# One projected tile's filler steps moved from the B heads into the A heads of an attention stage, on one Trainium2 core

## The chip, the cores and the metric

The kernel runs on one core of one Trainium2 chip. The metric is device time in microseconds (us) of one execution. Engines: TensorE (PE) multiplies matrices, VectorE (DVE) and ScalarE (ACT) do elementwise work and copies, GpSimd (POOL) adds and multiplies on the side, SyncE (SP) issues DMA loads and stores. PSUM is the memory that matmuls write, here eight banks.

## The reference, cut to what matters

One inference step of a one-layer encoder for 512 prompt frames and 64 new ones (576 tokens): a feed-forward network, an attention layer with two groups of heads, a second feed-forward network, a final norm.

```python
proj = u @ w_in                       # queries, keys, values of both groups
qa, ka, va, qb, kb, vb = jnp.split(proj, cuts, axis=-1)
qa, ka, qb, kb = rope(...)            # rotary
oa = swa_prompt(qa, ka, va, sinks)    # group A: chunk window, learned sinks
ob = diff_prompt(qb, kb, vb, lam)     # group B: softmax of map 1 - lam * softmax of map 2
h = h + jnp.concatenate([oa, ob], axis=-1) @ w_out
```

The 64 new frames do the same against a cache (`swa_sample`, `diff_sample`).

## The kernel before, in words

Products are exact to fp32 by three passes: each weight block is split into w_hi (a copy by ACT, `hi_block` L1334) and w_lo (a subtraction by DVE, `lo_block` L1855), and a step multiplies hi by hi, hi by lo and lo by hi for two halves of the tokens: six matmuls of 288 columns.

The projections of queries and keys are 13 tiles in the order ka, qa0 to qa3, kb0, qb0, kb1, qb1, kb2, qb2, kb3, qb3 (`TILES`, numbers 0 to 12), eight steps each (`tile_step` L1069). Every tile from qa1 on is accumulated in the same two PSUM banks. When a tile's eighth step is done, DVE takes it out (`take_projection` L2235: a shuffle, L2244, and a multiplication, L2246, which frees the banks); then POOL does the rotary (L2550, L2500) and, for a query tile, writes the new frames' part into a small tile q_diag (L2580). So:

- the first step of tile b waits until DVE has taken tile b - 1 (L1081);
- the take of tile b waits until POOL has finished the rotary of tile b - 1 (L2242), because both use the same two buffers;
- a rotary that writes into a slot waits until all scores that read the slot's former tile are made: q and k slots go by the head's number, even or odd (L2564), q_diag's two slots by the tile's number, even or odd (L2574 to L2577);
- the scores of a head wait for its tiles' rotary.

The attention is made of units: for each A pair t the units (A,t,0), (A,t,1) for the prompt and (As,t,0) for the new frames; for each B head h (Bs,h,0), (B,h,0) to (B,h,3), and L(Lh,0), which turns the head's output back. A unit is scored on PE (S), its maxima are found on DVE (`maxima` L2282), exponentials are made on ACT (`exps` L1691), probabilities are scaled on DVE (N, `normalise` L2318). Then it goes through one or two of 40 rounds, numbered 0 to 39: in round r PE transposes the probabilities (T r), ACT copies them (`copy_turned` L1723), and PE multiplies them with the values (O r). T r waits for the copy of T r-1. Rounds 0 to 19 are the A pairs (five for each: two for each A unit, one for As), rounds 20 to 39 the B heads. The outputs of an A pair are put by DVE into the mixing tiles (`outputs` L2352); B heads have a norm (R), scaled by ACT (L1775) before L.

Between these PE does filler steps, of the tiles first and then of the output projection. `make_schedule` (L254) writes all this as one list of events, which every engine follows in its own program order, so an instruction that waits holds all that stands behind it on that engine. `FILL` (L68) has for each round the number of steps after T r and its scores, and after O r; `FILL_START` (L67) the steps before round 0. `ACT_SPLITS` and `DVE_SPLITS` (L69, L70) say how many events of other kinds after the first step of tile b - 2 (or block) the w_hi and w_lo of block b stand. A few units' exponentials come late (`ACT_LATE`, L82): those of (A,2,0) stand behind the copy of T9.

SP loads each tile's 512 KB of weights into one of three slots, when the split of the block three before is done; stores of the rotated keys stand in the same queue, that of kb0 between the loads of qb1 and kb2, that of kb1 between those of qb2 and kb3, that of kb2 after that of qb3.

Of the kernel before, what the change touches and what calls it, by code (L numbers as in the profile page):

```python
# [63 lines left out]


LEAD = 2
FILL_START = (1, 6)  # L67
FILL = ((1, 0), (2, 0), (3, 0), (3, 0), (1, 4), (1, 0), (1, 0), (1, 0), (3, 0), (0, 3), (1, 0), (0, 0), (1, 0), (0, 3), (3, 0), (1, 1), (0, 3), (2, 1), (2, 0), (3, 3), (0, 2), (0, 2), (4, 2), (0, 5), (3, 0), (1, 2), (3, 2), (4, 2), (2, 0), (3, 1), (0, 0), (2, 2), (3, 0), (0, 1), (3, 0), (1, 1), (2, 1), (1, 3), (4, 0), (3, 9))  # L68
ACT_SPLITS = (4, 0, 4, 0, 0, 0, 2, 1, 3, 0, 3, 0, 7, 2, 0, 7)  # L69
DVE_SPLITS = (7, 17, 8, 6, 8, 0, 4, 2, 4, 10, 8, 0, 9, 9, 1, 21)  # L70
ACT_ROOTS = (1, 0, 0, 0)
ACT_SCALES = (0, 2, 2, 0)
ACT_TILES = (0, 0, 0, 3)
# [180 lines left out]
def make_schedule():  # L254
# [24 lines left out]
    def fill(n):  # L279

        for _ in range(n):
            step()

    def score(n):
        kind, t, _ = units[n]
        last = TILES.index(f"qa{t}" if kind[0] == "A" else f"qb{t}")

        while done[0] < (last + 1) * KD + (LEAD if n > 1 else 0) and step():
            pass
        events.append(("S", n))  # L290
# [3 lines left out]
    score(0)  # L294
    fill(FILL_START[0])
    score(1)
    events.append(("N", 0))
    fill(FILL_START[1])
    waiting = []
    for at, n in enumerate(scored):  # L300
        kind, head, i = units[n]
        parts = 2 if kind == "A" else 1
        for part in range(parts):
# [3 lines left out]
            if part == parts - 1:  # L307
# [4 lines left out]
                if at + 2 < len(scored) and at not in SCORES_FIRST:  # L312
                    score(scored[at + 2])
            fill(FILL[r][0])
            events.append(("O", r))
            fill(FILL[r][1])

# [17 lines left out]
def with_splits(places):  # L335

    out, owed = [], []
    for e in EVENTS:
        if e[0] == "k" and e[2] == 0 and e[1] <= LAST_FILLER:
            while owed and owed[0][0] < e[1] + 1:  # L340
                out.append(("W", owed.pop(0)[0]))
        out.append(e)
        if e[0] == "k":
            if e[2] == 0 and FIRST_TILES <= e[1] <= LAST_FILLER:
                owed.append([e[1] + 2, places[e[1] - FIRST_TILES]])
        else:
            for w in owed:
                w[1] -= 1
        while owed and owed[0][1] <= 0:
            out.append(("W", owed.pop(0)[0]))  # L350
    return out + [("W", b) for b, _ in owed]


def with_first_split(events):

    at = events.index(("N", 0)) + 1
    return events[:at] + [("W", V_BLOCKS - 1)] + events[at:]


def with_roots(events, later):  # L360

    out, held = [], []
    for e in events:
        if e[0] == "R":
            held.append([e, later[UNITS[e[1]][1]]])
        else:
            out.append(e)
            if e[0] not in "kW":
                for h in held:
                    h[1] -= 1  # L370
        while held and held[0][1] <= 0:
            out.append(held.pop(0)[0])
    return out


def with_scales(events, later):

    out, held = [], []
    for e in events:
        out.append(e)  # L380
        if e[0] == "R":
            held.append([("Q", e[1]), later[UNITS[e[1]][1]]])
        elif e[0] not in "kW":
            for h in held:
                h[1] -= 1
        while held and held[0][1] <= 0:
            out.append(held.pop(0)[0])
    return out


def with_late_scores(events, late):

    out, held = [], []
    for e in events:
        if e[0] == "S" and e[1] in late:
            held.append(e)
            continue
        out.append(e)
        if e[0] == "T":
            out += held  # L400
            held = []
    return out


ACT_EVENTS = with_scales(with_late_scores(with_roots(with_splits(ACT_SPLITS), ACT_ROOTS), ACT_LATE), ACT_SCALES)
DVE_EVENTS = with_first_split(with_roots(with_splits(DVE_SPLITS), DVE_ROOTS))

# [2333 lines left out]
```

## Time and profile before

| | us |
|---|---|
| median of 3 runs | 1033.09 (1032.91 to 1033.96) |
| the profiled execution | 1034.29 |
| its span, first to last instruction | 1032.5 |
| PE busy | 1015.2 (98%) |
| DVE busy | 799.8 (77%) |
| ACT busy | 564.5 (55%) |
| POOL busy | 171.6 (17%) |

Starts are counted from the first instruction of the span. A row of a timeline gives the start, the time from there to the end of the row's last instruction, engine, line, operation, output and inputs, and how many instructions it merges; a bracket at its end says how long the engine idled before it and whose end it waited for. Matmuls overlap, so a row's time is longer than the distance to the next row.

### The profile page before, as it was taken

The page shows a single profiled execution, that of the slowest core. Times are in us where ns is not written, and L with a number is a line of the kernel's source. Part 1 is how long each engine was busy: PE and PEld are TensorE (multiplying, and loading weights), DVE is VectorE, ACT ScalarE, POOL GpSimd, SP SyncE. Part 2 cuts the span into 40 slices and gives each one's busy share as a digit, 9 for nine tenths or more (in the row PEclk, how much of TensorE's full clock was granted, in tenths as well). Part 3 has the DMA queues.
Part 4 walks back from the last instruction along what each step waited for, and adds up shares of the span by engine and source line. Part 5 has one row for each costly group of instructions (what it writes and reads, how often), then busy time and mean ns, then how long its engine had stood idle before and what let it go on. Part 6 is the DMA issues. An engine that isn't in the chain of part 4 may idle for free.

```text
span 1032.5 us, 19489 instructions
## 1 busy us (share of the span) xinstructions
PE 1015.2 (98%) x7600; PEld 989.2 (96%) x7600; DVE 799.8 (77%) x1222; ACT 564.5 (55%) x980; POOL 171.6 (17%) x296
## 2 busy tenths in 40 slices
PE   9999999999999999999999999999999999999996
PEld 9999999999999999988888899999999999999995
DVE  6998777888678895368767768698777788778884
ACT  6645554666456663345435646435654666555664
POOL 0000010010010035233544205000000010010023
PEclk9999999999999999999999999999999999999999
DMA  6436656656665536230112212316556656667542
GB/s 231 110 95 155 190 149 166 186 149 158 177 176 149 139 121 211 64 97 22 52 54 70 83 57 82 106 56 185 166 148 162 183 152 169 176 156 179 143 106 92
DMA packets 38890, 137.33 MB, mean 133 GB/s; under 512 B 5456, under 2 KB 8656, under 8 KB 38672
## 3 DMA queue, kind: packets, MB, share of 16 engines
q1 hardware_dynamic: 30736, 107.52, 30.1%
q0 software_dynamic: 8064, 28.58, 17.3%
q8 instruction: 61, 1.00, 0.4%
q14 instruction: 29, 0.24, 0.1%
HBM read 131.10 MB, written 4.98 MB: 132 GB/s over the span
## 4 chain that ended last, share of the span: by engine, by line
PE 51%; DVE 5%; issue 3%; ACT 1%; POOL 1%; DMA 1%; DVEq 0%; SPq 0%; ACTq 0%; POOLq 0%
PE acc L985 25%; PE acc L883 17%; PE acc L1120 3%; PE acc L1156 1%; PE acc L1226 1%; DVE w_lo L1853 1%; PE acc L1146 1%; DVE h_lo L1988 1%; DMA comb<-in_w2se 0%; POOL side L2520 0%; DMA raw<-in_w2se 0%; DVE res L2469 0%; POOL q_b L2500 0%; PE acc L1185 0%; PE acc L1189 0%
## 5 line engine op out<-in xcount | busy, mean ns | idle before, releaser
L985 PE MATMUL acc<-c_hi,w_lo 128*128 128x288 f32 x952 | 282.0, 296 | 0.0
L985 PE MATMUL acc<-c_hi,w_hi 128*128 128x288 f32 x952 | 281.0, 295 | 0.0
L985 PE MATMUL acc<-c_lo,w_hi 128*128 128x288 f32 x952 | 277.6, 292 | 0.0
L1853 DVE TENSOR_TENSOR w_lo<-raw,w_hi 128x1024 fp32r<-128x1024 f32 (+4 forms) x187 | 196.5, 1053 | 103.4 <-ACT w_hi L1332 87.5
L1332 ACT ACTIVATE w_hi<-raw 128x1024 fp32r<-128x1024 f32 (+4 forms) x157 | 140.7, 896 | 88.0 <-PE acc L985 57.3
L1502 ACT ACTIVATE comb<-acc 128x288 f32<-128x288 f32 x224 | 92.1, 411 | 167.3 <-PE acc L985 165.0
L985 PEld LDWEIGHTS acc<-c_lo,w_hi 128*128 128x128 f32 x952 | 180.8, 190 | 0.0
L985 PEld LDWEIGHTS acc<-c_hi,w_hi 128*128 128x128 f32 x952 | 179.0, 188 | 0.2 <-DVE w_lo L1853 0.2
L985 PEld LDWEIGHTS acc<-c_hi,w_lo 128*128 128x128 f32 x952 | 178.5, 188 | 0.0
L985 PE MATMUL acc<-h_hi,w_hi 128*128 128x288 f32 x574 | 170.8, 298 | 2.3 <-DVE h_lo L1988 0.8
L985 PE MATMUL acc<-h_hi,w_lo 128*128 128x288 f32 x574 | 169.8, 296 | 0.0
L985 PE MATMUL acc<-h_lo,w_hi 128*128 128x288 f32 x574 | 167.9, 292 | 0.0
L1853 DVE TENSOR_TENSOR w_lo<-comb,w_hi 128x1024 fp32r<-128x1024 f32 (+2 forms) x86 | 101.4, 1179 | 18.1 <-ACT w_hi L1350 15.8
L985 PEld LDWEIGHTS acc<-h_hi,w_hi 128*128 128x128 f32 x574 | 108.0, 188 | 4.8 <-DVE h_lo L1988 1.7
L985 PEld LDWEIGHTS acc<-h_lo,w_hi 128*128 128x128 f32 x574 | 108.8, 190 | 0.0
L985 PEld LDWEIGHTS acc<-h_hi,w_lo 128*128 128x128 f32 x574 | 107.8, 188 | 0.0
L883 PE MATMUL acc<-h_hi,w_hi 128*128 128x288 f32 x320 | 69.1, 297 | 0.0
L883 PE MATMUL acc<-h_hi,w_lo 128*128 128x288 f32 x320 | 68.6, 295 | 0.0
L883 PE MATMUL acc<-h_lo,w_hi 128*128 128x288 f32 x320 | 68.5, 295 | 0.0
L1356 ACT ACTIVATE w_hi<-comb 128x1024 fp32r<-128x1024 f32 (+1 forms) x56 | 58.1, 1037 | 8.3 <-PE acc L985 7.0
L2520 POOL TENSOR_TENSOR side<-side 128x576 f32<-128x576 f32 x23 | 39.6, 1720 | 81.1 <-issue 50.9
L883 PEld LDWEIGHTS acc<-h_hi,w_hi 128*128 128x128 f32 x320 | 51.8, 188 | 0.2
(257 smaller groups left out, 1831.4 us busy)
## 6 DMA issues: line engine op xcount, KB each, us to landing
raw<-in_w1st SPq DMA_DIRECT2D x17, 768.0 KB, 4.6
raw<-in_w2st SPq DMA_DIRECT2D x17, 768.0 KB, 4.3
raw<-in_w_qk SPq DMA_DIRECT2D x13, 512.0 KB, 3.7
raw<-in_w1sd SPq DMA_DIRECT2D x8, 768.0 KB, 4.2
raw<-in_w2sd SPq DMA_DIRECT2D x8, 768.0 KB, 4.3
raw<-in_w1gu SPq DMA_DIRECT2D x10, 512.0 KB, 4.6
raw<-in_w2gu SPq DMA_DIRECT2D x10, 512.0 KB, 3.8
raw<-in_w1st SPq DMA_DIRECT2D x9, 512.0 KB, 5.3
```

Source lines behind the costliest of these rows:

```text
L883: m = nc.tensor.matmul(acc[:, bank + t, 0:HALF], w_part[:, col:col + P], x_part[:, k, t * HALF:(t + 1) * HALF], start=first and n == 0, st ...
L985: m = nc.tensor.matmul(acc[:, banks[side_of(p)], 0:HALF], w_part[:, col:col + P], x_part, start=n in (P1, P5, P2) and k == 0 and e == 0, s ...
L1120: m = nc.tensor.matmul(acc[0:n_tok, V_BANK[tt], 0:V_HALF], x_part[:, kg, tok], w_part[:, split_base(key) + k * V_HALF:split_base(key) + (k ...
L1146: m = nc.tensor.matmul(acc[:, bank + e, 256 * qi + (P if tile == 0 else 0):256 * (qi + 1)], q_a[rows, t % 2, tile * P:(tile + 1) * P], k_a ...
L1156: m = nc.tensor.matmul(acc[:, bank + e, 0:(i + 1) * P], q_b[rows, t % 2, i * P:(i + 1) * P], k_b[rows, t % 2, 0:(i + 1) * P], start=True, ...
L1226: m = nc.tensor.matmul(acc[:, O_BANK, i * P:(i + 1) * P], pt[:, j * P:(j + 1) * P], v_new[:, j, b_values(t)], start=j == 0, stop=j == i)
L1332: nc.scalar.activation(cols, src, ACT.Copy).then_inc(hi_ready, 1)
L1356: nc.scalar.activation(parts_of(w_hi, P6, P3 - P6, p), w_sum[:, :, 0:width(p)], ACT.Copy).then_inc(hi_ready, 1)
L1502: nc.scalar.activation(to, acc[:, PRODUCTS[n][0][side_of(p)], 0:HALF], ACT.Copy, scale=scale).then_inc(snapped, 1)
L1853: return nc.vector.tensor_tensor(cols, src, hi.bitcast(FP32), ALU.subtract).then_inc(split_ready, 1)
L1988: nc.vector.tensor_tensor(pair_lo[:, at:at + n, :], side[:, 0:n, :], pair_hi[:, at:at + n, :].bitcast(FP32), ALU.subtract).then_inc(h_read ...
L2520: nc.gpsimd.tensor_tensor(ssq[:], ssq[:], square, ALU.add).then_inc(ssq_added, 1)
```

## The change

Eight filler steps move: `FILL_START` gets one step more and round 0 one less (qa1's last step goes ahead of T0); round 8 gets eight steps, all after O8, in place of three ahead of it; rounds 10, 11 and 12 get one more each; round 15 does its two ahead of O15; rounds 22, 23 and 26 lose three, two and three. Every tile from kb0 to kb3 ends at another place than before. Where the tile steps stand after the change, with the first steps of the next tile behind them:

```
T8 S(A2,0) O8 kb0.0-7 T9 S(A2,1) O9 qb0.0-2 T10 qb0.3-4 T11 S(As2,0) qb0.5 O11 T12 qb0.6-7
T13 S(A3,0) O13 kb1.0-2 T14 S(A3,1) kb1.3-5 O14 T15 kb1.6-7 T16 S(As3,0) O16 qb1.0-2 T17 qb1.3-4 qb1.5
T18 S(Bs0,0) qb1.6-7 O18 T19 S(B0,0) kb2.0-2 O19 kb2.3-5 T20 S(B0,1) O20 kb2.6-7 T21 S(B0,2) O21 qb2.0-1
T22 S(B0,3) qb2.2-3 O22 qb2.4 T23 S(Bs1,0) O23 qb2.5-7 T24 S(B1,0) kb3.0-2 O24 T25 S(B1,1) kb3.3 O25 kb3.4-5
T26 S(B1,2) kb3.6-7 O26 L(L0,0) T27 ...
```

From T27 on PE's list is the same as before. The w_hi of qb1 on ACT now stands between the exponentials of (A2,1) and the copy of T10. On DVE the w_lo of qb0 stands behind the take of qa3, that of kb1 ahead of the take of kb0, that of qb1 between the mixing outputs of O13 and the maxima of (A3,1), that of kb2 behind the maxima of (As3,0), that of qb2 ahead of the probabilities of (Bs0,0), that of kb3 behind the maxima of (B0,2), that of qb3 behind O24.

```diff
-FILL_START = (1, 6)
-FILL = ((1, 0), (2, 0), (3, 0), (3, 0), (1, 4), (1, 0), (1, 0), (1, 0), (3, 0), (0, 3), (1, 0), (0, 0), (1, 0), (0, 3), (3, 0), (1, 1), (0, 3), (2, 1), (2, 0), (3, 3), (0, 2), (0, 2), (4, 2), (0, 5), (3, 0), (1, 2), (3, 2), (4, 2), (2, 0), (3, 1), (0, 0), (2, 2), (3, 0), (0, 1), (3, 0), (1, 1), (2, 1), (1, 3), (4, 0), (3, 9))
+FILL_START = (1, 7)
+FILL = ((0, 0), (2, 0), (3, 0), (3, 0), (1, 4), (1, 0), (1, 0), (1, 0), (0, 8), (0, 3), (2, 0), (1, 0), (2, 0), (0, 3), (3, 0), (2, 0), (0, 3), (2, 1), (2, 0), (3, 3), (0, 2), (0, 2), (2, 1), (0, 3), (3, 0), (1, 2), (2, 0), (4, 2), (2, 0), (3, 1), (0, 0), (2, 2), (3, 0), (0, 1), (3, 0), (1, 1), (2, 1), (1, 3), (4, 0), (3, 9))
 ACT_SPLITS = (4, 0, 4, 0, 0, 0, 2, 1, 3, 0, 3, 0, 7, 2, 0, 7)
-DVE_SPLITS = (7, 17, 8, 6, 8, 0, 4, 2, 4, 10, 8, 0, 9, 9, 1, 21)
+DVE_SPLITS = (7, 17, 10, 0, 12, 10, 6, 8, 12, 14, 8, 0, 9, 9, 1, 21)
```

## Rows read from the trace of the kernel before

**Rows 1.** The page, part 1: busy time, share of the span and instructions.

```profile
PE 1015.2 (98%) x7600; PEld 989.2 (96%) x7600; DVE 799.8 (77%) x1222; ACT 564.5 (55%) x980; POOL 171.6 (17%) x296
```

**Rows 2.** The table of stretches: length, engines' busy time, PE's clock, DMA.

```profile
441.00:560.00 119.00, 114.76 (x902) 100.10 (x900) 91.04 (x234) 55.63 (x171) 52.49 (x150) 1.00 0.19 64
```

**Rows 3.** PE's timeline, rounds 1 to 18.

```profile
452.26 0.51 PE L883 MATMUL acc<-u_hi,w_hi 128*128 128x288 f32 x2 [0.91 <-DVE side L2246]
...
475.49 0.51 PE L883 MATMUL acc<-u_hi,w_hi 128*128 128x288 f32 x2 [0.16 <-DVE side L2246]
...
479.09 0.33 PE L1181 MATMUL acc<-ident,probs 128*128 128x128 f32 x1
...
484.04 0.55 PE L1178 MATMUL acc<-ident,probs 128*128 128x128 f32 x3 [0.23 <-DVE probs L2332]
...
485.63 0.52 PE L1178 MATMUL acc<-ident,probs 128*128 128x128 f32 x3 [0.25 <-ACT probs_t L1733]
...
489.42 0.63 PE L1178 MATMUL acc<-ident,probs 128*128 128x128 f32 x4 [0.43 <-ACT probs_t L1733]
...
499.25 0.55 PE L1178 MATMUL acc<-ident,probs 128*128 128x128 f32 x3 [0.46 <-DVE probs L2332]
...
501.23 0.49 PE L1178 MATMUL acc<-ident,probs 128*128 128x128 f32 x3
501.56 0.49 PE L1151 MATMUL acc<-k_all_a,q_diag 128*128 128x192 f32 x2
...
503.11 0.53 PE L883 MATMUL acc<-u_hi,w_hi 128*128 128x288 f32 x2
...
508.17 0.43 PE L883 MATMUL acc<-u_hi,w_lo 128*128 128x288 f32 x2
508.44 0.60 PE L1178 MATMUL acc<-ident,probs 128*128 128x128 f32 x4
509.90 1.24 PE L1160 MATMUL acc<-k_all_b,q_diag 128*128 128x288 f32 x4 [0.86 <-POOL q_diag L2580]
```

**Rows 4.** PE's timeline, rounds 24 to 27: T24 and a step, T26 and T27.

```profile
540.72 0.60 PE L1185 MATMUL acc<-ident,probs 128*128 128x128 f32 x4
...
541.66 0.54 PE L883 MATMUL acc<-u_hi,w_hi 128*128 128x288 f32 x2
...
550.47 0.27 PE L1185 MATMUL acc<-ident,probs 128*128 128x128 f32 x1
...
556.39 0.38 PE L1185 MATMUL acc<-ident,probs 128*128 128x128 f32 x2
```

**Rows 5.** DVE's timeline: takes, maxima, and probabilities without and beside POOL's rotary.

```profile
450.68 0.80 DVE L2244 STREAM_SHUFFLE side<-acc 128x576 f32<-128x576 f32 x1
451.37 0.74 DVE L2246 TENSOR_TENSOR side<-acc,trig 128x576 f32<-128x576 f32 x1
...
489.03 0.81 DVE L2244 STREAM_SHUFFLE side<-acc 128x576 f32<-128x576 f32 x1
...
495.95 0.27 DVE L2292 MEMSET acc<- 64x256 f32 x1 [0.40 <-PE acc L1146]
...
498.58 1.14 DVE L2332 TENSOR_SCALAR probs<-probs,st 128x256 f32<-128x256 f32 x4
...
503.38 1.79 DVE L2332 TENSOR_SCALAR probs<-probs,st 128x256 f32<-128x256 f32 x4
```

**Rows 6.** DVE's splits of tiles' weights, 441 to 560: duration in ns, least/median/most.

```profile
L1853 DVE TENSOR_TENSOR w_lo<-raw,w_hi x10: 1210/1220/1412, 448.8 to 545.7; 128x1024 fp32r<-128x1024 f32 x10
```

**Rows 7.** ACT's timeline: a w_hi split, and the scaling of head 0.

```profile
496.17 1.07 ACT L1332 ACTIVATE w_hi<-raw 128x1024 fp32r<-128x1024 f32 x1
...
552.30 1.57 ACT L1775 ACTIVATE o_b<-o_b,ss_o 128x128 f32<-128x128 f32 x5 [0.71 <-DVE ss_o L2388]
```

**Rows 8.** POOL's timeline: the rotary of qb0.

```profile
502.38 2.24 POOL L2550 TENSOR_TENSOR side<-side,trig 128x96 f32<-128x96 f32 x6 [7.61 <-DVE side L2244]
...
509.14 0.71 POOL L2580 TENSOR_TENSOR q_diag<-side 64x64 f32<-64x64 f32 x2
```

## The prediction

> **What bounds the kernel now.** I read the page first: TensorE is busy for 98% of the span [rows 1], so time can come only out of its idle spells, and go only into new ones. The table of stretches puts them in one place: between 441 and 560 us, where the attention rounds run between filler steps, PE is busy for 114.76 of 119.00 us [rows 2]. That leaves 4.24 us, the most that any order of the steps can win there. Then I read PE's timeline through this stretch [rows 3, 4] for the bracket behind a row, which says how long PE idled before it and what ended that. The reader should see three kinds of idle: a tile's first step waits until DVE has taken the former tile out of its banks (452.26, 475.49); a transpose waits for ACT's copy of the transpose before (485.63, 489.42) or for DVE's probabilities (484.04, 499.25); and one score waits for POOL's rotary (509.90). Last I read DVE, ACT and POOL at these places [rows 5 to 8]. All clocks there are granted at 1.00 [rows 2].
>
> **What moves.** Steps are dear only where they fill nothing. Two matmuls start 0.27 us apart (508.17 to 508.44) [rows 3], so a step of six costs 0.80. All 104 tile steps stay; rounds 8 (+5), 10, 11 and 12 (+1 each) get eight, rounds 22 (-3), 23 (-2) and 26 (-3) lose them. From kb0 on each tile therefore ends at another round, and with it moves everything that a tile issues: ACT's w_hi, DVE's w_lo and its two instructions of the take, POOL's fifteen pieces, SP's load. I write +x for "x us after the row that begins the round's transposes".
>
> **Gains**, each from an idle spell that a step now covers.
> (a) qa1's last step goes ahead of T0. Its take (two instructions, 450.68 to 452.11, 1.43 us [rows 5]) starts about 0.3 earlier, and qa2's wait of 0.91 [rows 3] shrinks by as much; it does not end, since T1 now waits for the copy of T0. Gain 0.3.
> (b) O8 goes between qa3's end and kb0's first step: the wait of 0.16 at 475.49 [rows 3] and a change between kinds of matmul go. Gain 0.25.
> (c) From T11 to T13 two more steps cover the copies' latencies (0.43 of idle at 489.42). T11 to T13 took 3.79 (485.63 to 489.42) [rows 3]; the work without waits, with two steps more, comes to about 4.5, in place of 3.79 + 1.6. Gain 0.9, at least the 0.43 of the idle spell.
> (d) qb0's rotary is now early, so S(Bs0,0) no longer stands 0.86 for POOL's q_diag [rows 3]. Gain 0.85.
> Together 2.3; bounds 1.7 (c at its least) and 2.7 (PE's idle at these places and what the kinds' changes add).
>
> **Losses.**
> (e) T9 to T11. T11 already waits for ACT, whose copy of T10 stands behind the exponentials. qb1's w_hi comes ahead of that copy now: a row of 1.07, about 0.95 of it not overlapped [rows 7]. One step more lies beside it. Also kb0's rotary now runs on POOL while DVE makes the probabilities of (A2,0). The four scalings took 1.14 with POOL idle and 1.79 beside POOL's rotary [rows 5, 8], 0.16 more each; with the small instructions before them I take 0.26 for ACT's start. So T9 to T11 goes from 6.54 [rows 3] to 7.75, where the step alone would make 7.34. Loss 0.4; bounds 0 (ACT's work hides) and 1.0 (no cover).
> By the Trainium skill (SBUF — State Buffer, section Who interferes with whom) the port pair of VectorE and GpSimd is an exclusive lock for a whole instruction; a scaling would then stand out a whole piece of POOL, an estimate of 2.24/6 = 0.37 in place of 0.16 [rows 8], and the time would be some 0.4 longer than my sum.
> (f) T13 to T15. DVE's chain from the take at 489.03 to its idle at 495.55 (0.40 before the row at 495.95) is 6.52 long [rows 5]: take, probabilities, maxima, mixing outputs. Before, it began 0.4 ahead of T13; now qb0 ends right at T13, so it begins at +0.2. And qb1's w_lo (1.22 in the median [rows 6], of which the next overlaps little) stands behind it, ahead of the maxima of (A3,1). They start at +7.9, not +6.53 (495.95 - 489.42). T15 waits for what follows from them (it idled 0.46 there already [rows 3]). Loss 1.3; bounds 0.9 (no extra start) and 1.5.
> (g) T16, the largest. q_diag has two slots, by the tile's number; POOL may write qb0's only when S(As3,0), a user of qa3's, is scored. Before, qb0 was taken at T16, and the score long done when POOL came to it at 509.14 [rows 8]. Now POOL has rotated qb0 by about +7 of round 13 and stands until S(As3,0), which follows T16. kb1 ends right before T16, its take waits for qb0's rotary to be done, and qb1's first step waits for that take. S(As3,0) ends at +0.82 (501.56 + 0.49 - 501.23) [rows 3]; POOL begins some 0.14 later, q_diag takes 0.71 [rows 8], the take begins 0.1 later and lasts 1.43, and PE starts 0.15 after it (452.11 to 452.26) [rows 3, 5]: +3.35. Without the wait the step would start at +1.88, as kb1.0 did (503.11) [rows 3]. Queued behind the take on DVE are the probabilities of (A3,1), which T17 needs; three steps of qb1 hide them. Loss 1.5; bounds 1.2 and 1.8.
> (h) T24. qb2 ends right there, and kb3 starts after T24 and S(B1,0) alone, at +0.94 (540.72 to 541.66) [rows 4], where qb2 used to go on. It needs qb2's take: +0.2, 1.43, 0.15, so +1.8. Loss 0.85; bounds 0.6 and 0.9.
> (i) T26. Three steps less before T27, but the transposes L(L0,0) need ACT's scaling, done at 552.30 + 1.57 [rows 7], +3.4. With 0.14 and 0.55 for them T27 is at +4.1, where 5.92 [rows 4] less 2.4 makes 3.5. POOL is quieter there after the change, and DVE's norm before ACT's scaling shorter. Loss 0.45; bounds 0 and 0.65.
> Together 4.5; bounds 2.7 and 5.8.
>
> At nothing: rounds 22 and 23. Without their steps T23 and T24 still come after the probabilities of (B0,2) and (B0,3), T24 by only 0.4, which is the cover to lose. SP loads kb2 and qb2 earlier, since the store of kb0 ahead of them waits for kb0's rotary; kb3's load waits for kb1's and lands some 4 us before ACT comes to it. POOL holds kb2 until S(B0,3), over 6 us before qb2's take needs it. Only where a landing is later than this does ACT's copy, queued behind w_hi, make PE wait.
>
> **The sum.** 4.5 - 2.3 = 2.2 longer. The profiled execution took 1034.29 with a span of 1032.5; the changed one would be 1036.5 with 1034.7. That execution lies 1.2 above the median of the runs, 1033.09; from the median I get **1035.3**. A measurement of this kernel can tell about 0.2%, 2.07 us, from no change, so the line of slower is 1035.16.
>
> **Rivals.**
> Slower by more: the DVE queue before kb0's end has no slack. qb0's w_lo moves behind the take of qa3, kb1's ahead of the take of kb0, and by my addition it ends within 0.1 of where that take is due. One split later, and take, maxima, probabilities of (A2,0) and T10 all shift by up to 1.2: 1036.5. For it: the w_lo rows reach 1.41 [rows 6], and DVE is the engine behind T10. It decides from the point where kb1's w_lo ends later than T9 + 0.2. Chance 0.17.
> Not slower: q_diag's turn is no hold. If the take at T16 found qb0 rotated, (g) is 0 and the rest is 0.7: 1033.8. The code's wait speaks against it; that POOL showed this wait nowhere before speaks neither way. It decides if S(As3,0) is scored 1.5 us ahead of where I place it. Chance 0.18.
> Faster: DVE's and POOL's holds both vanish in slack that I missed, (f), (g) and (h) are 0. Less (e) and (i) that is 2.3 - 0.85, or 1031.6; with these two at their lower bound too it is 1030.8. PE's idle of 4.24 allows it. Chance 0.10.
>
> **How the numbers follow.** My forecast has the other 0.55, and the line of slower cuts it nearly in half. Slower: 0.31 of it and 0.16 of the first rival, 0.47. Same: 0.24 of it, all of the 0.18 but 0.01, 0.01 of the first rival and 0.02 of the last, 0.44 in all. Faster: the 0.08 left of the last and that 0.01, 0.09. Bounds alone give 2.7 - 2.7 = 0 to 5.8 - 1.7 = 4.1, so 1033.1 to 1037.2; I take the lower end to 1032.4 for part of the second rival.
>
> **What would show it.** Right: an idle of about 1.5 before the first qb1 step behind O16, ended by DVE's take; POOL's q_diag of qb0 right behind S(As3,0); about 1.7 before T15; 0.85 before kb3's first step; no wait before S(Bs0,0); no gap before T13. Wrong: the qb1 step starting at +1.9, or PE's idle between 441 and 560 under 5 us.

## The result, and the profile after

The changed kernel takes 1036.52 us (median of 12 runs, 1034.90 to 1038.66), the kernel before in the same comparison 1033.72 us (12 runs, 1032.91 to 1034.35). The ratio is 1.0029, interval 1.0020 to 1.0038: slower by 2.1 to 3.9 us. The forecast was 1035.3, a loss of 2.2 us on a median of 1033.09. Of the 1.22 us between forecast and result, 0.63 lies in the base alone, whose median was 1033.72 this time. The other 0.6 is the matter of this part.

The profiled execution of the changed kernel took 1037.19 us, with a span of 1035.4. Its page, part 1, answers to [rows 1]:

```profile
PE 1015.8 (98%) x7600; PEld 990.4 (96%) x7600; DVE 800.1 (77%) x1222; ACT 564.5 (55%) x980; POOL 172.2 (17%) x296
```

As many instructions as before. The span is 2.9 us longer and PE only 0.6 us busier, so most of the loss shows as idle time. The table of stretches shows where, beside [rows 2] (length, busy time of PE, PEld, DVE, ACT and POOL, granted clock, DMA share, GB/s):

```profile
441.00:560.00 119.00, 112.04 (x878) 98.80 (x876) 87.02 (x228) 54.67 (x169) 50.32 (x141) 0.99 0.20 64
```

PE idles for 6.96 us here where it idled for 4.24, and the granted clock beside it is 0.99, not 1.00. The table of waits for PE from 441 to 565 us names what ended the idle spells (total us, times, longest):

```profile
PE acc L1178 <- DVE probs L2332: 2.8, 2, 1.9
PE acc L883 <- DVE side L2246: 2.5, 3, 1.4
PE acc L1178 <- ACT probs_t L1733: 1.0, 2, 0.7
PE acc L1245 <- ACT o_b L1775: 0.3, 1, 0.3
```

The two longest are the two that the prediction priced highest: probabilities before T15 (part f) and a tile's take before qb1's first step (part g). POOL's q_diag wait of [rows 3] is gone from the list (part d). PE's timeline, in order:

```profile
441.16 0.93 PE L1146 MATMUL acc<-k_a,q_a 64*128 64x128 f32 x8
...
473.15 0.63 PE L1178 MATMUL acc<-ident,probs 128*128 128x128 f32 x4
...
482.09 0.27 PE L1181 MATMUL acc<-ident,probs 128*128 128x128 f32 x1
...
487.43 0.55 PE L1178 MATMUL acc<-ident,probs 128*128 128x128 f32 x3 [0.91 <-DVE probs L2332]
...
489.91 0.52 PE L1178 MATMUL acc<-ident,probs 128*128 128x128 f32 x3 [0.34 <-ACT probs_t L1733]
...
494.37 0.60 PE L1178 MATMUL acc<-ident,probs 128*128 128x128 f32 x4
...
505.63 0.55 PE L1178 MATMUL acc<-ident,probs 128*128 128x128 f32 x3 [1.91 <-DVE probs L2332]
...
507.61 0.49 PE L1178 MATMUL acc<-ident,probs 128*128 128x128 f32 x3
...
510.99 0.52 PE L883 MATMUL acc<-u_hi,w_hi 128*128 128x288 f32 x2 [1.44 <-DVE side L2246]
...
514.98 0.60 PE L1178 MATMUL acc<-ident,probs 128*128 128x128 f32 x4
...
517.82 0.60 PE L1178 MATMUL acc<-ident,probs 128*128 128x128 f32 x4
518.25 1.14 PE L1160 MATMUL acc<-k_all_b,q_diag 128*128 128x288 f32 x4
...
544.95 0.60 PE L1185 MATMUL acc<-ident,probs 128*128 128x128 f32 x4
...
546.74 0.51 PE L883 MATMUL acc<-u_hi,w_hi 128*128 128x288 f32 x2 [0.76 <-DVE side L2246]
...
555.49 0.27 PE L1185 MATMUL acc<-ident,probs 128*128 128x128 f32 x1
...
558.93 0.63 PE L1245 MATMUL acc<-ident,o_b 128*128 128x128 f32 x4 [0.31 <-ACT o_b L1775]
...
559.50 0.38 PE L1185 MATMUL acc<-ident,probs 128*128 128x128 f32 x2
...
566.45 0.49 PE L1185 MATMUL acc<-ident,probs 128*128 128x128 f32 x3
```

These are S(A0,0), T8, T9, T10, T11, T13, T15, T16, qb1's first step, T17, T18, S(Bs0,0), T24, kb3's first step, T26, L(L0,0), T27 and T28. Three rows of the kernel before are needed beside them, S(A0,0), T17 and T28:

```profile
441.52 0.93 PE L1146 MATMUL acc<-k_a,q_a 64*128 64x128 f32 x8
...
505.60 0.60 PE L1178 MATMUL acc<-ident,probs 128*128 128x128 f32 x4
...
563.10 0.49 PE L1185 MATMUL acc<-ident,probs 128*128 128x128 f32 x3
```

The wait before T15 goes back to DVE, where qb1's w_lo now stands right ahead of the maxima of (A3,1) (the first of their instructions is the one at 502.34):

```profile
501.01 1.21 DVE L1853 TENSOR_TENSOR w_lo<-raw,w_hi 128x1024 fp32r<-128x1024 f32 x1
502.34 0.27 DVE L2292 MEMSET acc<- 64x256 f32 x1
```

The chain behind the row at 510.99 is to be seen on POOL and DVE, a row of each:

```profile
508.57 0.70 POOL L2580 TENSOR_TENSOR q_diag<-side 64x64 f32<-64x64 f32 x2 [8.55 <-PE acc L1151]
```

```profile
509.39 0.01 DVE L2244 LOAD_MASK_SELECT side<-acc  x1 [2.89 <-POOL q_diag L2580]
509.41 0.80 DVE L2244 STREAM_SHUFFLE side<-acc 128x576 f32<-128x576 f32 x1
```

POOL stood 8.55 us for the scores of S(As3,0) (L1151), wrote qb0's q_diag, and only then did DVE take kb1, after standing for 2.89 us itself; PE got its banks 1.6 us later. That is part (g), link by link.

Each interval of the stage can now be read against its term. The last column is gain (+) or loss (-) against [rows 3, 4], with 0.80 per step that came or went:

| part, interval | predicted us | measured us | measured gain or loss |
|---|---|---|---|
| b: T8 to T9, five steps more | 8.99 | 8.94 | +0.30 |
| e: T9 to T11, one step more | 7.75 | 7.82 | -0.48 |
| c: T11 to T13, two steps more | 4.5 | 4.46 | +0.93 |
| f: T13 to T15 | 11.1 | 11.26 | -1.43 |
| g: T16 to qb1's first step | 3.35 | 3.38 | -1.50 |
| d: T18 to S(Bs0,0) | 0.60 | 0.43 | +1.03 |
| h: T24 to kb3's first step | 1.8 | 1.79 | -0.85 |
| i: T26 to T27, three steps fewer | 4.1 | 4.01 | -0.49 |

Part (a), from S(A0,0) to T2, gained 0.33 where 0.3 stood. The whole stage from S(A0,0) to T28 took 566.45 - 441.16 = 125.29 us; before, 563.10 - 441.52 = 121.58. That is 3.71 longer, and the sum of the prediction explains 2.2 of it. The missing 1.5 sits in one interval for which it had no term: qb1's three steps, from 510.99 to T17 at 514.98, took 3.99 us. The same three steps of kb1 had taken 505.60 - 503.11 = 2.49 before. The table of stretches by single microseconds says why (the column after POOL's count is the granted clock):

```profile
509.00:510.00 1.00, 0.55 (x11) 0.31 (x6) 0.60 (x2) 0.00 (x0) 0.28 (x1) 1.00 0.00 0
510.00:511.00 1.00, 0.01 (x1) 0.04 (x1) 1.00 (x3) 0.00 (x0) 0.65 (x2) 1.00 0.00 0
511.00:512.00 1.00, 1.00 (x5) 1.00 (x6) 0.93 (x4) 0.00 (x0) 1.00 (x4) 0.68 0.03 8
512.00:513.00 1.00, 1.00 (x6) 1.00 (x6) 1.00 (x3) 0.00 (x0) 0.92 (x4) 0.50 0.07 16
513.00:514.00 1.00, 1.00 (x6) 1.00 (x6) 0.93 (x5) 0.00 (x0) 1.00 (x4) 0.50 0.00 0
514.00:515.00 1.00, 1.00 (x7) 1.00 (x7) 1.00 (x1) 0.00 (x0) 1.00 (x1) 0.61 0.00 0
515.00:516.00 1.00, 1.00 (x11) 1.00 (x9) 0.01 (x1) 0.38 (x1) 1.00 (x5) 1.00 0.00 0
```

PE is called busy for all of 511 to 515, but at a granted clock down to 0.50, its lower level of 1.2 GHz; five or six matmuls begin in each of the first three microseconds there, eleven in the one at 1.00. PE had idled 1.91 us before T15 and 1.44 us before qb1 just ahead of it. By the Trainium skill (TensorE: Matmul & The Clock Gate, section What's actually happening) the clock is set by how busy PE has lately been; this trace agrees, with idle spells of 1.91 and 1.44 us ahead of the fall.

Each run also lists its mean granted clock. Of the twelve, the four at 0.998 took 1034.90 to 1035.76, the eight at 0.994 to 0.997 took 1036.23 to 1038.66. (What else enters this mean is told in the last part.)

### The profile page after: what moved, and what is told of

It is laid out like the page before. It is cut to its first block, busy times and chain, and to the rows that moved or that the text cites. A ratio compares the mean times of both kernels' runs of the same rounds, so it can differ in the third digit from the quotient of the medians.

```text
span 1035.4 us, 19489 instructions
## 1 busy us (share of the span) xinstructions
PE 1015.8 (98%) x7600; PEld 990.4 (96%) x7600; DVE 800.1 (77%) x1222; ACT 564.5 (55%) x980; POOL 172.2 (17%) x296
## 4 chain that ended last, share of the span: by engine, by line
PE 56%; DVE 3%; ACT 2%; issue 1%; POOL 1%; DVEq 0%; ACTq 0%; POOLq 0%
PE acc L985 28%; PE acc L883 18%; PE acc L1120 3%; PE acc L1156 1%; PE acc L1226 1%; PE acc L1178 1%; PE acc L998 1%; PE acc L1212 1%; PE acc L1146 0%; POOL side L2520 0%; DVE res L2469 0%; PE acc L1189 0%; DVE side L2244 0%; PE acc L1230 0%; PE acc L1160 0%
```

## The experiments

Two questions were left. Are the waits of (f) and (g) what their chains say, and what are they worth singly? And does the half clock come from PE's idle spells, and from which? The first four kernels shared their runs of the kernel before (1033.21, 32 runs), the last four theirs (1033.28, 23 runs). A whole run can't tell half a microsecond, so I read the stage beside it: S(A0,0) to T28 of each profiled execution, against 121.58 before. Outside this stage the profiled executions differ by up to 1.7 us, from 909.6 (the kernel of E3: span 1030.7 less 121.14) to 911.3 (E1: 1033.6 less 122.29), where no step was moved. The stage is that of one execution, the median that of all: the medians of E1 and E2 lie 1.40 and 1.66 us over the kernel before, their stages 0.71 and 1.06. No profile shows where this difference comes from.

**E1: qb0 gets a slot of q_diag of its own** (a free piece of another buffer), so part (g) is undone alone.

```diff
+        def diag_slot(b):
+            return 2 if TILES[b] == "qb0" else b % 2
...
-                        before = [n for c in range(b) if TILES[c][0] == "q" and c % 2 == b % 2
+                        before = [n for c in range(b) if TILES[c][0] == "q" and diag_slot(c) == diag_slot(b)
```

> The changed kernel, with a third q_diag slot of its own for qb0, so that POOL need not wait for S(As3,0) and DVE's take of kb1 is not held (step g alone undone). Theory 1 (the loss is made of single waits, each at its place, and of matmuls at half clock right behind them): the first qb1 step starts 1.9 us after T16's row, not 3.4; T15 still idles 1.9; the clock stays 1.00 between T16 and T18, since the second idle spell is gone; time 0.7 us above the kernel before (ratio 1.0007; 1.3 above if the clock falls now and then from T15's spell alone). Rival (DVE has too little time in the A half, so that its delay shows at the next wait whichever is removed): the 1.5 us turn up before T17 or S(Bs0,0), ratio 1.002 or more.

Measured: 1034.61 us, ratio 1.0014 [1.0006, 1.0023]. The wait before qb1's first step is gone, T15's stays, and T15 to T17 took 6.36 (506.03 to 512.39) in place of 9.35, 1.5 less by the wait and 1.5 by the clock:

```profile
506.03 0.55 PE L1184 MATMUL acc<-ident,probs 128*128 128x128 f32 x3 [1.90 <-DVE probs L2338]
...
509.08 0.88 PE L1218 MATMUL acc<-probs_t,v_new 128*64 128x128 f32 x12 [0.25 <-ACT probs_t L1739]
```

The stage took 563.88 - 441.59 = 122.29, 0.71 over before, which is the forecast of 2.2 less (g)'s 1.5. The slot's turn is what held POOL.

**E2: qb1's w_lo four events later in DVE's order**, behind the mixing outputs of O14, so part (f) is undone alone.

```diff
-DVE_SPLITS = (7, 17, 10, 0, 12, 10, 6, 8, 12, 14, 8, 0, 9, 9, 1, 21)
+DVE_SPLITS = (7, 17, 10, 0, 16, 10, 6, 8, 12, 14, 8, 0, 9, 9, 1, 21)
```

> The changed kernel with DVE's w_lo of qb1 moved from ahead of the maxima of (A3,1) to behind the outputs of O14, where DVE stands still for 2.9 us (step f alone undone). Theory 1: T13 to T15 falls from 11.26 us to 10.0, T15's idle from 1.9 to 0.7; the wait of the first qb1 step stays at 1.4 us (it hangs on S(As3,0), not on DVE's load); the clock stays 1.00 behind it, since one spell alone does not bring it down; time 0.9 us above the kernel before (ratio 1.0009). Rival (DVE's load): T15 earlier, but the split shows later, at T17 or T18, ratio 1.002 or more. Rival on the clock (one spell of 1.4 is enough): half clock behind it in the profile, ratio 1.0015 or more.

Measured: 1034.87 us, ratio 1.0015 [1.0006, 1.0024].

```profile
504.26 0.55 PE L1178 MATMUL acc<-ident,probs 128*128 128x128 f32 x3 [0.77 <-DVE probs L2332]
...
509.62 0.51 PE L883 MATMUL acc<-u_hi,w_hi 128*128 128x288 f32 x2 [1.44 <-DVE side L2246]
```

T15's wait falls from 1.91 to 0.77, by 1.14; the rest of (f), some 0.3, is the take of qb0, whose place the edit leaves: the maxima of (A3,1) begin 6.82 behind T13 (500.96 - 494.14) where 6.53 stood before. The stage took 563.57 - 440.93 = 122.64, 1.06 over before. The profiled execution kept the clock at 1.00, but four runs of 11 list 0.996 and took 1035.39 to 1035.63, the other seven 1034.33 to 1034.92.

**E3: both edits.**

> The changed kernel with both edits, the third q_diag slot and the later w_lo of qb1 (steps f and g undone, e, h and i left). Theory 1, by the terms: 4.5 - 1.3 - 1.5 = 1.7 of losses against 2.3 of gains, 0.6 us below the kernel before (ratio 0.9994), clock 1.00 throughout rounds 15 to 18, PE idle between 441 and 560 about 3.5 us. Rival (filling the A half gains nothing by itself, since DVE's chain is the bound there): not below the kernel before, ratio 1.000 to 1.002.

Measured: 1032.62 us, ratio 0.9997 [0.9988, 1.0006]; the stage took 561.70 - 440.56 = 121.14, 0.44 less than before. With (f) mostly and (g) wholly gone, the gains win. The two parts add up, so neither hid behind the other: against E4 below, the changed kernel with the clock kept, the stage is shorter by 1.49 in E1, 1.14 in E2 and 2.64 in E3. Here are the waits that are left:

```profile
PE acc L1184 <- DVE probs L2338: 1.7, 2, 0.9
PE acc L889 <- DVE side L2252: 1.0, 2, 0.8
PE acc L1184 <- ACT probs_t L1739: 1.0, 2, 0.7
PE acc L1251 <- ACT o_b L1781: 0.3, 1, 0.3
```

**E4: PE kept busy through both spells of the changed kernel**, eleven matmuls whose result nobody reads before T15 and nine before qb1's first step. Nothing that PE waits for comes sooner.

```diff
+                if event == ("T", 15):
+                    keep_busy(11)
+                if event == ("k", 8, 0):
+                    keep_busy(9)
```

> The changed kernel with matmuls of no use (128x288, into the bank of the transposes): eleven ahead of T15, about 1.5 us, and nine ahead of the first qb1 step, about 1.2 us; all waits stay as they are. If the half clock behind the first qb1 step comes from PE's idle spells there, it is gone: three steps of qb1 take 2.5 us, not 4.0, the time is 2.2 us above the kernel before (ratio 1.0021) and its runs lie within 1.5 us of each other, not 3.8. If the clock falls for another reason, the half clock stays in some runs and the time is 2.8 to 3.5 us above.

Measured: 1035.44 us, ratio 1.0022 [1.0013, 1.0031], ten runs from 1034.92 to 1036.05.

```profile
508.96 1.45 PE L1301 MATMUL acc<-u_hi 128*128 128x288 f32 x9
510.49 0.50 PE L883 MATMUL acc<-u_hi,w_hi 128*128 128x288 f32 x2
...
512.96 0.60 PE L1178 MATMUL acc<-ident,probs 128*128 128x128 f32 x4
```

The first step still starts 3.40 behind T16 (507.09), but the three steps take 2.47 (510.49 to 512.96) instead of 3.99; T15 still comes 11.27 behind T13 (493.84 to 505.11). The stage took 564.42 - 440.64 = 123.78: 2.20 over before, as much as the forecast's net. The runs spread over 1.1 us where the changed kernel's spread over 3.8, and no mean clock lies under 0.997. Work that does nothing makes the stage 1.5 us shorter than the changed kernel's, by keeping the clock. One profile could be chance, as four of the changed kernel's twelve executions kept a mean clock of 0.998; but none of the ten runs here took longer than 1036.05, and eight of those twelve did. This is the experiment on which the cause of the missing term rests. The ratios alone (1.0022 and 1.0029, with overlapping intervals) would not settle it.

**E5: E3 with rounds 22 to 26 filled otherwise**, against parts (h) and (i): qb2's last step goes behind T24, so O24, T25 and S(B1,1) come between qb2's take and kb3's first step, and five steps lie between T26 and L(L0,0).

```diff
-... (0, 2), (2, 1), (0, 3), (3, 0), (1, 2), (2, 0), (4, 2), ...
+... (0, 2), (2, 0), (0, 3), (1, 0), (1, 2), (3, 2), (4, 2), ...
```

> As e3_both, and rounds 22 to 26 filled otherwise: 22 loses its step after O22, 24 keeps one of its three, and 26 gets three more, so qb2's last step and O24, T25 and S(B1,1) stand between qb2's take and kb3's first step, and five steps between T26 and L(L0,0). Theory (parts h and i are real and separate from f and g): the waits of 0.77 before kb3's first step and of 0.31 before L(L0,0) go, about 1.0 shorter than e3_both's 1032.6, so 1031.6 where the kernel before takes 1033.2, ratio 0.9985. Rival (these waits cover something else, T24's probabilities or O24's copy, that waits in their place): no gain over e3_both, ratio 0.9996, with a new idle spell at T24 or O24.

Measured: 1031.78 us, ratio 0.9988 [0.9979, 0.9997]: faster than the kernel before. kb3's first step and L(L0,0) start without a wait, as the missing brackets show:

```profile
544.77 0.53 PE L889 MATMUL acc<-u_hi,w_hi 128*128 128x288 f32 x2
...
553.75 0.60 PE L1251 MATMUL acc<-ident,o_b 128*128 128x128 f32 x4
```

The stage took 561.01 - 441.36 = 119.65, 1.49 less than E3's. The rival expected a wait at T24 or O24; in this trace neither has one. Parts (h) and (i) are real and separate from (f) and (g); with the wait of S(B1,3) that went too they make 0.85 + 0.49 + 0.24 = 1.58. E5 undoes them together, so what each is worth alone is read from the changed kernel's rows only.

**E6: E5 with qb1's w_hi on ACT behind the copy of T10**, against part (e).

```diff
-ACT_SPLITS = (4, 0, 4, 0, 0, 0, 2, 1, 3, 0, 3, 0, 7, 2, 0, 7)
+ACT_SPLITS = (4, 0, 4, 0, 2, 0, 2, 1, 3, 0, 3, 0, 7, 2, 0, 7)
```

> As e5_refill, and qb1's w_hi on ACT goes behind the copy of T10 instead of ahead of it. Theory (part e is ACT's queue): the idle spell of 0.33 before T11 goes, T9 to T11 comes down from 7.8 to about 7.4, 0.3 shorter than e5_refill: ratio 0.9982. Rival (T9 to T11 is long because of DVE beside POOL, not because of ACT's queue): T11 as late as before, ratio as e5_refill's.

Measured: 1031.84 us, ratio 0.9986 [0.9977, 0.9995]. ACT's timeline shows the two in the new order:

```profile
487.59 0.50 ACT L1739 ACTIVATE probs_t<-acc 128x384 f32<-128x384 f32 x1
487.96 1.08 ACT L1338 ACTIVATE w_hi<-raw 128x1024 fp32r<-128x1024 f32 x1
```

T9 to T11 took 488.70 - 481.38 = 7.32 and T11 has no wait, so ACT's order alone gives back all of (e)'s 0.48. It isn't the only thing in it: T10 still comes 5.34 behind T9, as in the changed kernel, where 4.95 stood before. The stage took 559.61 - 440.44 = 119.17, 2.41 less than before and 0.48 less than E5's. The median doesn't show it (1031.84 against 1031.78): half a microsecond is below what these runs can tell.

**E7 and E8: one spell kept busy, the other left**, E4's edit with one of its two parts. First E7, which leaves the spell before qb1:

> The changed kernel with eleven matmuls whose result nobody reads ahead of T15 only, so that PE stands still for 1.4 us before qb1's first step but not for 1.9 us before T15. Theory (the two spells together bring the clock down): granted clock 1.00 through both, only the net wait of 2.2 us stays, ratio 1.0021 with a spread of the runs near 1 us, as e4_kept_busy. Rival (the spell right ahead of the slow steps does it alone): clock 0.5 after qb1's first step, ratio 1.0028 or more, runs spread over 2 to 4 us.

Measured: 1036.19 us, ratio 1.0027 [1.0016, 1.0039], six runs from 1035.04 to 1037.45. E8 leaves the spell before T15:

> The changed kernel with nine matmuls whose result nobody reads ahead of qb1's first step only, so that PE stands still for 1.9 us before T15 but not for 1.4 us before qb1. Theory (the two spells together bring the clock down): clock 1.00, ratio 1.0021, spread near 1 us. Rival (the longer spell does it alone): the clock falls to 0.5 behind T15 or around qb1's first step, ratio 1.0028 or more, runs spread over 2 to 4 us.

Measured: 1036.08 us, ratio 1.0029 [1.0018, 1.0041], six runs from 1035.67 to 1038.72. Both profiled executions kept the clock through the stage (E7's stretches behind its first qb1 step):

```profile
511.00:512.00 1.00, 1.00 (x9) 1.00 (x8) 1.00 (x3) 0.00 (x0) 1.00 (x3) 1.00 0.09 25
```

and both stages took 123.76, the 2.2 of the waits and no more. The runs tell another story. In E7 three at 0.998 took 1035.04 to 1035.40, and three at 0.996 took 1036.98 to 1037.45: two groups, 1.6 us apart at the least. In E8 one of six lists 0.995 and took 1038.72, the others 0.997 to 0.998 and 1035.67 to 1036.28. So the theory that it takes both spells does not hold: with the 1.4 us before qb1 left alone, three of six runs here and four of 11 of E2 list a lower mean clock and are longer. For the 1.9 us before T15 left alone the evidence is thin: one run of six here, while of E1, which leaves the same spell, the three runs at 0.996 are no longer than its others. With neither left (E4) no run of ten was longer. All this is read from times and mean clocks; no profile caught the clock falling behind a single spell.

## Why the prediction was right, and where it was short

**The intervals.** All eight came within 0.17 us of the forecast, (g) and (h) within 0.03. They came out of one trace because each was built as a chain: what frees the engine, in which order its queue stands, and how long each instruction takes in a row.

**The largest terms, (f) and (g).** Their mechanisms are shown by E1 to E3, which undo them singly and together. On (f), the maxima of (A3,1) began at 502.34, 7.97 behind T13, where 7.9 stood. On (g), the rival that q_diag's turn is no hold fell: POOL's 8.55 us are that hold.

**The rival of no slack before kb0's end** was a near miss: kb1's w_lo ended at 482.14, and DVE began the take at 482.30 after standing 0.17 for PE. A split later by the 0.19 between the median and the longest of [rows 6] would have used that up; the 1.2 of that rival would have taken a whole split more ahead of the take.

**Part (e)** was 0.48 and not 0.4, close in part by luck. Of DVE beside POOL: kb0's rotary did run beside the probabilities of (A2,0), and T10 came 5.34 behind T9 where 4.95 stood before, so 0.39 later; the prediction had 0.26 for what this does to ACT's start. But the four scalings took 1.34, 0.05 more each than the 1.14 they take with POOL idle, not the 0.16 that I took from [rows 5]. Two small instructions before them grew instead, from 0.16 each to 0.29 and 0.25, and the maxima ahead of these began 0.12 later behind T9. E6 wins the 0.48 back with T10 as late as that, since T11 then follows T10 by 1.98 without a wait, where the 1.59 of before and a step would make 2.39: the step now covers a wait for ACT's copy that stood there before (0.25 in [rows 3]). The rule of the exclusive lock (the Trainium skill, SBUF — State Buffer, section Who interferes with whom), which is stated there for VectorE's 2-port modes, gave an estimate of 0.37 for each scaling. The trace shows no such wait: single scalings took 0.36 to 0.41 where 0.35 stood. In which mode they ran no run here shows. The reduction ahead of the scalings took 1.22 while POOL's rotary ran, as without it before (1.23).

**Part (d)** was 1.03, not 0.85 (1.12 up to T19): more went than the wait of 0.86 itself. **What had no term:** S(B1,3) stands 0.16 for the probabilities on ACT behind the scaling, so T27 to T28 took 6.95 where 6.71 stood. Gains of 0.33 + 0.30 + 0.93 + 1.12 = 2.7 and losses of 0.48 + 1.43 + 1.50 + 0.85 + 0.49 + 0.24 = 5.0 took the place of the 2.3 and 4.5 forecast, and what lies between these intervals came 0.1 shorter: the small errors cancelled, and that the net stayed at 2.2 to the tenth is luck. A slip without effect: the least of the gains is 1.83 by its own terms (0.3 + 0.25 + 0.43 + 0.85), not 1.7, so the range's upper end should stand 0.1 lower.

**The step that failed** is "All clocks there are granted at 1.00" as a reading of the stage, carried over to the changed kernel without saying so. The prediction put new idle spells of 1.4 and 1.9 us close together and priced each at its own length. In the profiled execution they cost 1.5 us more, since qb1's three steps ran at half the clock. In the median that term is about 1036.52 - (1033.72 + 2.2) = 0.6: the four runs at 0.998 lie 1.2 to 2.0 us over the base, the other eight 2.5 to 4.9. It also explains the spread of the runs, which the prediction did not foresee. "PE's idle under 5 us" as the mark of a wrong forecast was well chosen but blind to this: at half clock PE counts as busy.

## What to carry to other kernels

Price a new wait on PE twice: its own length, and what the work behind it costs if the granted clock falls after it. When moving a step, follow what its tile's end triggers in each other engine's queue; here the gains of 2.7 us were real, and were lost to one weight split ahead of a maximum and one buffer whose turn had come too late. Undoing just these, and refilling three rounds, made the same change 1.5 us faster than the kernel before (E5; 0.3 to 2.2 by its interval). And where an effect is under the noise of whole runs, read the stage between two fixed events of the trace: it repeated to 0.02 us in three executions that kept the clock and had the same waits there (E4, E7, E8), while the rest of their spans differs by 0.5, and that of all ten profiles by 1.7.

## What the runs showed of the hardware

The granted clock fell to 0.50 between 511 and 515 us, after PE had idled for 1.91 and 1.44 us with about 4 us of work and short waits between, and came back while PE worked on without a gap. Whether it falls there seems to differ between executions of the same program: the changed kernel's runs list mean clocks from 0.994 to 0.998, and the lower ones are longer. Before, the longest spell in the stage was 0.91 us, and the runs of the kernel before list 0.997 or 0.998 in all 55 executions of the two experiments' comparisons.

The mean clock of a run is a blurred sign of this, for every profile here, that of before too, shows the clock at 0.50 at the end of the span as well, where PE's last matmul is done and the clock costs nothing:

```profile
1020.00:1032.50 12.50, 3.35 (x15) 2.15 (x14) 5.55 (x13) 2.97 (x7) 3.77 (x5) 0.80 0.54 189
```

That alone makes 0.998 of 1.00 in this execution (0.20 of 12.5 us out of 1032.5). When it begins differs: at 1023.8 of 1030.4 us in E5's profile, at 1030 of 1033.9 in E8's. Half clock from the last matmul's end on (1024.6 in before's profile) would give 0.996, an estimate from these rows. So a run at 0.996 that is no longer than others needs no fall in the stage, which can explain the three of E1 (1034.67 to 1035.08, where the others reach 1035.38); 0.995 and 0.994 need a fall elsewhere too.

One thing stays open. Two runs of E5 list 0.996 and took 1033.65 and 1034.05, nearly 2 us and more above the others' middle, though the longest spell in its profile is 0.91 in the stage and 1.1 in the whole span, as in the kernel before; what made them longer no profile shows.
